# Reading x first, conditioning sums in four column groups on TensorE, and cact placed in front of x

## The reference

```
c_act = jax.nn.silu(c)
for l in range(DEPTH):
    mod = jnp.einsum('bd,kde->kbe', c_act, ada_w[l]) + ada_b[l][:, None, :]
    sh1, sc1, gt1 = jnp.split(mod[0], 3, axis=-1)
    sh2, sc2, gt2 = jnp.split(mod[1], 3, axis=-1)
    h = modulate(x, norm_mix_g[l], sh1, sc1)      # rmsnorm(x, g) * (1 + scale) + shift
    x = x + gt1[:, None, :] * token_mixer(h, ...)
    h = modulate(x, norm_ffn_g[l], sh2, sc2)
    x = x + gt2[:, None, :] * (swiglu or moe_ffn)(h, ...)
return rmsnorm(x, final_norm_g)
```

## Time and profile before

| | us |
|---|---|
| median of 3 runs | 1609.29 (1606.48 to 1611.79) |
| profiled execution | 1608.77 |
| its span, first to last instruction | 1606.8 |
| mean granted TensorE clock | 0.977 |
| PE busy | 1534.2 |
| DVE busy | 1174.7 |
| ACT busy | 785.8 |

### The profile page before, as it was taken

How to read it: one execution, slowest core, us unless ns; L and a number is a source line. 1 busy time by engine, 2 the same in 40 slices (tenths; PEclk the granted TensorE clock), 3 DMA queues, 4 the chain that set the end, 5 groups by cost and what they waited for, 6 DMA issues and landing times.

```text
span 1606.8 us, 22402 instructions
## 1 busy us (share of the span) xinstructions
PE 1534.2 (95%) x8920; PEld 1212.1 (75%) x8920; DVE 1174.7 (73%) x1451; ACT 785.8 (49%) x919; POOL 61.5 (4%) x49
## 2 busy tenths in 40 slices
PE   6899999999999999998999999799999999999993
PEld 6567877777888888886678768588888888888883
DVE  6777876766666565546578764589989998998994
ACT  2444236332222222214542463477777777777774
POOL 8200000000000000000000000100000000000001
PEclk9999999989999999999999999899999999999996
DMA  8362211436555564531211005299999999999975
GB/s 344 105 236 81 93 53 54 157 131 185 183 183 183 181 193 147 184 109 53 62 46 53 27 28 185 90 379 405 388 390 394 392 390 386 381 390 392 393 277 170
DMA packets 94454, 340.31 MB, mean 212 GB/s; under 512 B 10000, under 2 KB 14096, under 8 KB 91664
## 3 DMA queue, kind: packets, MB, share of 16 engines
q1 hardware_dynamic: 92048, 330.51, 56.8%
q0 software_dynamic: 2304, 8.39, 1.4%
HBM read 316.84 MB, written 22.02 MB: 211 GB/s over the span
## 4 chain that ended last, share of the span: by engine, by line
PE 90%; DVE 4%; DMA 2%; ACT 1%; issue 1%; POOL 0%; SPq 0%; POOLq 0%; ACTq 0%; DVEq 0%
PE ps L623 34%; PE ps L1194 10%; PE ps L1192 10%; PE ps L1193 10%; PE ps L924 2%; DMA scr<-in_ada 2%; DVE scr L1678 2%; PE ps L952 1%; PE ps L781 1%; PE ps L773 1%; PE ps L936 1%; PE ps L580 1%; PE ps L1034 1%; PE ps L636 1%; PE ps L1036 1%
## 5 line engine op out<-in xcount | busy, mean ns | idle before, releaser
L1675 DVE TENSOR_TENSOR wlm<-rawm,hlo 128x2048 fp32r<-128x2048 f32 x120 | 274.7, 2289 | 26.3 <-ACT hlo L1293 24.6
L1233 ACT ACTIVATE whi<-raw 128x1024 fp32r<-128x1024 f32 (+1 forms) x112 | 123.3, 1103 | 310.0 <-PE ps L623 265.1
L1293 ACT ACTIVATE hlo<-rawm 128x2048 fp32r<-128x2048 f32 x120 | 230.0, 1917 | 75.3 <-PE ps L1194 75.2
L623 PE MATMUL ps<-hhi,whi 128*128 128x512 f32 x624 | 257.0, 412 | 1.9 <-DVE wlo L1685 1.9
L1685 DVE TENSOR_TENSOR wlo<-raw,whi 128x1024 fp32r<-128x1024 f32 (+1 forms) x112 | 145.0, 1295 | 147.7 <-ACT whi L1233 145.4
L623 PE MATMUL ps<-hhi,wlo 128*128 128x512 f32 x624 | 247.1, 396 | 0.0
L623 PE MATMUL ps<-hlo,whi 128*128 128x512 f32 x624 | 246.1, 394 | 0.0
L1193 PE MATMUL ps<-wlm,xgh 128*128 128x512 f32 x480 | 187.7, 391 | 0.0
L1675 DVE TENSOR_TENSOR wlm<-rawm,whm 128x2048 fp32r<-128x2048 f32 x60 | 137.6, 2293 | 28.6 <-ACT whm L1293 28.6
L623 PEld LDWEIGHTS ps<-hhi,whi 128*128 128x128 f32 x624 | 117.9, 189 | 41.0 <-issue 12.8
L1192 PE MATMUL ps<-hlo,xgh 128*128 128x512 f32 x360 | 143.5, 399 | 0.6 <-issue 0.6
(11 more groups left out here) (315 smaller groups left out, 2553.0 us busy)
## 6 DMA issues: line engine op xcount, KB each, us to landing
rawm<-in_wm SPq DMA_DIRECT2D x360, 512.0 KB, 7.3
raw<-in_w SPq DMA_DIRECT2D x96, 512.0 KB, 3.6
adah<-in_ada SPq DMA_DIRECT2D x56, 512.0 KB, 4.3
scr<-in_ada SPq DMA_DIRECT2D x20, 1024.0 KB, 5.9
raw<-in_w SPq DMA_DIRECT2D x16, 704.0 KB, 4.1
xs<-scr SPq DMA_DIRECT2D x15, 512.0 KB, 5.4
ys<-yb SPq DMA_DIRECT2D x15, 512.0 KB, 8.4
xg<-xs SPq DMA_DIRECT2D x14, 512.0 KB, 7.0
```

Source lines behind the costliest of these rows:

```text
L623: ins = pe.matmul(ps[:, b, :], a, r[:, k0 + k, :], start=(start and first and k == ks[0] and n == 0), stop=(stop and last and k == ks[-1] ...
L1233: act.activation(whi[:, slot, 0:width], raw[:, slot, 0:width], ACT.Copy).then_inc(sem("hi_ready"), 1)
L1293: act.activation(hi_pair(q), raw_pair(q), ACT.Copy).then_inc(sem("him_ready"), 1)
L1675: return dve.tensor_tensor(out, a, b, op)
```

## The change

1. The first constants (identity, ones, and two columns moved to the front, `pick`, which is 1 on every 32nd partition, and `eps`) and `x` are issued ahead of the ada groups; all eight ada groups have buffers of their own and follow without a wait; the rest of the constants comes behind weight tiles 0 and 1. What reads those waits for `cst_in` at 32.
2. All eight groups are summed on PE. `condition_rows` multiplies with the stationary operand a column of `cact` repeated 32 times and the moving operand 256 columns of `ada`; chunk `k` goes to column group `k % 4`, so that the four partial sums stand on partitions 0-31, 32-63, 64-95 and 96-127 of one bank. ACT copies the bank to SBUF, and `condition_sum` turns and sums it with `pick` (two fp32 matmuls of one column).
3. DVE adds the squares of chunks 0 to 6 pairwise (`square_added`); PE sums only the last two. Then DVE makes `x*rstd` for all chunks ahead of `mod`. Scale and shift follow together: ACT makes `hhi` from `h` with scale and bias, DVE makes the same value unrounded (`whole`) and subtracts `hhi`.
4. `cact` is allocated in front of `x` instead of behind `rstd`.
5. `ang_ready`, `tap0` and `tap1` are replaced by counts on other semaphores; the same instructions wait for the same ones.

```diff
-BY_PE = (0, 2, 5, G_GATE, G_FFN - 1)
+BY_PE = tuple(range(G_IN)) + (G_GATE, G_FFN - 1)
...
         par = sb("par", [N_PAR])
+        cact = sb("cact", [DC])
         x = sb("x", [DC, S])
...
         rstd = sb("rstd", [S])
-        cact = sb("cact", [DC])
...
+        def row_bank(g):
+            return ps[:, (3, 4, 5, 6, 0, 1, 3, 4)[g], 0:256]
+        def row_copy(g):
+            return scr[:, 4 * 1024 + g % 4 * 256:4 * 1024 + g % 4 * 256 + 256]
...
-            for g in range(G_IN - 1):
+            sp.dma_start(cst[:, 0:N_FIRST], consts[:, 0:N_FIRST]).then_inc(sem("cst_in"), 16)
+            sp.dma_start(x[:], xT.rearrange("(c p) s -> p c s", p=P)).then_inc(sem("x_in"), 16)
+            for g in range(G_IN):
                 load_ada(g)
-            sp.dma_start(cst[:, 0:N_CONST - 9], consts[:, 0:N_CONST - 9]).then_inc(sem("cst_in"), 16)
-            sp.dma_start(x[:], xT.rearrange("(c p) s -> p c s", p=P)).then_inc(sem("x_in"), 16)
-            load_ada(G_IN - 1)
             load_tile(0)
             load_tile(1)
+            sp.dma_start(cst[:, N_FIRST:N_CONST - 9], consts[:, N_FIRST:N_CONST - 9]).then_inc(sem("cst_in"), 16)
...
+            def condition_rows(g):
+                ada_landed(pe, g)
+                if g >= 6:
+                    pe.wait_ge(sem("ada_copied"), g - 5)
+                for k in range(DC):
+                    j = 32 * (k % 4)
+                    ins = pe.matmul(row_bank(g)[j:j + 32, :], cact[:, k:k + 1].broadcast_to([P, 32]),
+                                    adar(g)[:, k * 256:(k + 1) * 256], start=(k < 4), stop=(k >= 4))
+                ins.then_inc(sem("ada_rows"), 1)
+            def condition_sum(g):
+                pe.wait_ge(sem("ada_copied"), g + 1)
+                for m in range(2):
+                    ins = pe.matmul(ps[:, 7, 2 * g + m:2 * g + m + 1], row_copy(g)[:, m * P:m * P + P], C("pick"),
+                                    start=True, stop=True)
+                ins.then_inc(sem("ada_used"), 1)
...
-                    for g in BY_PE[:3]:
-                        ada_sum(g)
+                    pe.wait_ge(sem("cact_ready"), 1)
                     pe.wait_ge(sem("cst_in"), 16)
-                    for g in (1, 3):
-                        ada_sum(g)
-                    for k in range(DC):
-                        square_sum(0, k)
-                    for g in (4, 6, 7):
-                        ada_sum(g)
+                    for g in range(G_IN):
+                        condition_rows(g)
+                        if g == 2:
+                            summed_squares(0)
+                        if g:
+                            condition_sum(g - 1)
+                    condition_sum(G_IN - 1)
...
+            for g in range(G_IN):
+                act.wait_ge(sem("ada_rows"), g + 1)
+                if g >= 4:
+                    act.wait_ge(sem("ada_used"), g - 3)
+                act.activation(row_copy(g), row_bank(g), ACT.Copy).then_inc(sem("ada_copied"), 1)
+                if g == 2:
+                    rms(0)
             for g in range(2):
                 split(g)
-            rms(0)
...
-            for g in (1, 3, 4, 6, 7):
-                ada_groups((g,))
+            dve.wait_ge(sem("x_in"), 16)
+            for k in range(1, DC - 1):
+                square_added(0, k)
+            inverse(0)
+            for k in range(DC):
+                tt(h[:, k, :], x[:, k, :], rstd[:]).then_inc(sem("hn_ready"), 1)
             for g in range(2):
                 split(g)
             dve.wait_ge(sem("ada_used"), G_IN)
             modulation(0, 2 * G_IN, 0, 1)
-            inverse(0)
+            for k in range(DC):
+                whole = scr[:, 5 * 1024 + k * S:5 * 1024 + k * S + S]
+                link(dve.tensor_scalar(whole, h[:, k, :], sclg[:, 0, k:k + 1], mod[:, k:k + 1], ALU.mult, ALU.add))
+                dve.wait_ge(sem("hhi_ready"), k + 1)
+                tt(hlo[:, k, :], whole, hhi[:, k, :].bitcast(F32), ALU.subtract).then_inc(sem("h_ready"), 1)
```

More of the change, by code:

```diff
@@ L44 @@
 _at = 0
-for _n, _w in (("ident", 128), ("ones", 128), ("bones", 128), ("rot", 128), ("istk", 64), ("amask", 256),
+for _n, _w in (("ident", 128), ("ones", 128), ("pick", 1), ("eps", 1), ("bones", 128), ("rot", 128), ("istk", 64), ("amask", 256),
                ("lev", 6 * 64), ("reset", 512), ("rows", 512), ("spread", 8 * 64), ("selg", 256),
                ("heads", 4 * 8), ("comb_r", 8), ("comb_l", 8), ("col_r", 16), ("col_l", 16), ("col_g", 16),
-               ("sign", 1), ("qscale", 1), ("rotm", 1), ("nrotm", 1),
-               ("eps", 1), ("before", 128), ("blocks", 16 * 8), ("rank", 8), ("invf", 1)):
+               ("sign", 1), ("qscale", 1), ("rotm", 1), ("nrotm", 1), ("before", 128), ("blocks", 16 * 8), ("rank", 8), ("invf", 1)):
     C_COLS[_n] = (_at, _at + _w)
@@ L52 @@
 N_CONST = _at
+N_FIRST = C_COLS["eps"][1]
 P_COLS = {}
@@ L115, in constants @@
     put("ones", np.ones((P, P)))
+    put("pick", (p % 32 == 0)[:, None] * 1.0)
     same = (p[:, None] // 64 == p[None, :] // 64)
@@ L395, in load_ada @@
                     sp.wait_ge(sem("sincos"), 2)
-                if g == 7:
-                    sp.wait_ge(sem("ada_used"), 1)
-                elif g == G_GATE + 2:
+                if g == G_GATE + 2:
                     sp.wait_ge(sem("ada_used"), G_GATE + 1)
@@ L553, in _ @@
                                         ALU.add, ALU.min))
-                pool.tensor_scalar(ang[:, n, :], ang[:, n, :], -float(np.float32(3.1415925)), None, ALU.max)\
-                    .then_inc(sem("ang_ready"), 1)
+                turn(pool.tensor_scalar(ang[:, n, :], ang[:, n, :], -float(np.float32(3.1415925)), None, ALU.max))
             pool.wait_ge(sem("xs_cleared"), 16 * NB)
@@ L895, in _ @@
                 for t in range(I_FILL):
+                    if t == 2:
+                        pe.wait_ge(sem("cst_in"), 32)
                     pe.wait_ge(sem(f"bank_free{t % 2}"), U_IN[layer] + t // 2)
@@ L1257, in shifted @@
                     shift = mod[:, s * 24 + k:s * 24 + k + 1]
-                    if s < 3:
+                    if s == 0:
+                        act.activation(hhi[:, k, :], h[:, k, :], ACT.Identity, scale=sclg[:, 0, k:k + 1], bias=shift)\
+                            .then_inc(sem("hhi_ready"), 1)
+                    elif s < 3:
                         act.activation(hhi[:, k, :], h[:, k, :], ACT.Identity, bias=shift).then_inc(sem("hhi_ready"), 1)
@@ L1416, in _ @@
                         if layer == 0:
-                            act.wait_ge(sem("ang_ready"), 2)
+                            act.wait_ge(sem("ang_step"), 2 + 2 * 13)
                             act.activation(sinb[:], ang[:, 2, :], ACT.Sin).then_inc(sem("sincos"), 1)
@@ L1726, in ada_first @@
                 if g >= 4:
-                    dve.wait_ge(sem("ada_used"), {4: 1, 6: 2, 7: 5}.get(g, max(G_IN, g - 3)))
+                    dve.wait_ge(sem("ada_used"), max(G_IN, g - 3))
                 return dve.tensor_scalar(adac[:, g % 4, :], w, cact[:, 0:1], None, ALU.mult)
@@ L1887, in _ @@
                     tap_list += [(d, 1)] + ([(d + lead, 0)] if d + lead < CV_K else [])
+                tap_at = {tap: n + 1 for n, tap in enumerate(tap_list)}
                 def taps(m):
@@ L1897, in taps @@
                         else:
-                            dve.wait_ge(sem(f"tap{n}"), CV_K * layer + d)
+                            dve.wait_ge(sem("tap"), 2 * CV_K * layer + tap_at[d - 1, n])
                             ins = stt(o[:, d:], src[:, :S - d], w, o[:, d:])
-                        ins.then_inc(sem(f"tap{n}"), 1)
+                        ins.then_inc(sem("tap"), 1)
                 def state(n):
@@ L2014, in _ @@
                         taps(2 * CV_K)
-                        for n in range(2):
-                            dve.wait_ge(sem(f"tap{n}"), CV_K * v)
+                        dve.wait_ge(sem("tap"), 2 * CV_K * v)
                         dve.sem_inc(sem("taps_done"), 1)
```

18 lines of the change are left out of this document (10 added, 8 removed).

## The result

| | before | after |
|---|---|---|
| median of the runs, us | 1610.60 (6 runs, 1606.48 to 1613.21) | 1598.42 (6 runs, 1593.27 to 1600.74) |
| ratio | | 0.9919, 95% interval 0.9905 to 0.9933 |
| profiled execution, its span | 1608.77, 1606.8 | 1593.27, 1591.2 |
| PE busy, us | 1534.2 | 1514.1 |
| TensorE clock granted, mean | 0.977 | 0.973 |

The change makes the kernel faster by 12.2 us, 0.8%. The forecast was 1584, that is 25 us faster; the time lies in its range (1577 to 1601), and the gain is a little less than half of what it said. The profiled execution after is the fastest of its six, so a comparison of the two profiles shows 15.5 us where the medians show 12.2.

The account below looks back on a forecast made before the run. The prediction took PE, busy 95% of the span, as the bound, with one long wait at the start. Its sum was 1608.8 - 8 (start) - 17 (address) = 1583.8, so 1584 us, range 1577 to 1601.

Parts of the forecast that it names:

- The start: Stretch up to `first_pair`: reordered transfers and sums on PE bring its first matmul to 42 instead of 50.2 us, gain 8.
- The pace of `first_pair`: In `first_pair`, behind the start: per chunk PE needs two triples, 1.40 us at full clock, and DVE 0.7 + 0.7.
- a rival: Conditioning sums at the start: column groups don't run together, 1601, or 1641 if PE also falls to half clock; chance 0.02.
- The weighing of the shared ports: DVE beside GpSimd at the start: trace shows slowing by a third to a half; full blocking would make the gain nearer 5.
- The address: Triples moving `hhi` or `hlo`: from byte 32 to 0 of 64 saves 20 ns each, 13.5 us plus 3.5, together 17.
- a term whose reason doesn't hold: Expert stage, 480 triples reading two of three moving operands from `hlo`: at most 6.4 us, half taken, 3.5.
- something else: Expert stage: whatever keeps `whm2`, at 0 of 64 already, at 0.69 a triple, not 0.68; it takes a part of the gain.
- the start alone: Whole kernel: the 20 ns belong to something else, such as a place above 100,000 bytes; 1601 us, chance 0.14.
- the one of the address alone: Whole kernel: DVE locked by POOL, or late products, leave at most 2 us of the start's gain; 1591 us, chance 0.06.
- the first case: Whole kernel: both gains, start and address, come; 1584 us, between 1577 and 1591, chance 0.76.
- The lines of 16 bytes: SBUF addresses 32224 and 32256: both are multiples of 16, so by the skill's rule the 32-byte shift brings nothing.

Follow-up runs that it names:

- start_only: The changed kernel with `cact` put back behind `rstd`, so new start and old address: 1600.11 us, ratio 0.9937.
- warm: The changed kernel with 15 matmuls added whose result nobody reads, to keep TensorE busy up to `first_pair`: 1600.54 us in one run.
- pool_late: The changed kernel with the second half of GpSimd's chain of angles held until both weight splits are done: 1600.29 us in one run.
- triples_idle: Bench of nothing but triples, operand addresses changed from group to group, other engines idle: 700 ns at the addresses before, 697 after, 680 at those of `ghi` and `glo`.
- addr_only: The kernel before with only `cact` moved in front of `x`, old start kept: 1603.80 us, ratio 0.9950.
- the repeat: The changed kernel as it is, measured once more on the same chip: 1597.85 us, ratio 0.9911.
- aligned: The changed kernel with `sclg` (128 bytes) put in front of `x` too: 1582.33 us, ratio 0.9818.

## Why the prediction was right and wrong

**The start: right.** Forecast were the first matmul at about 42 (bounds 39.3 to 45) and a gain of 8; measured 41.83 and 8.4. In `start_only` they are 41.03 and 9.2, with 8.7 left at 90 us, and its median says 11.4 with an interval from 6 to 14. The parts: squares begin at 12.3 (forecast: `x` there at 12.2), rows of a group 1.07 us (1.0) and `condition_sum` 0.5 to 0.6 (0.5) at full clock, copy 0.38 (0.4), both splits 3.70 (3.75). Two terms were off and cancelled. The last ada group's rows ended only at 34.5 instead of 33.6, since the clock was at half from 29.7 on and they took 1.91 us, where I had 1.0; and from the end of the splits to the first matmul it took 2.3 us, where I had 3.2. That they cancelled was luck. The pace of `first_pair` was off too: the prediction gave DVE 1.4 us a chunk, and it takes 2.3 with GpSimd beside it (`warm`). The clock I had not put into this stretch at all, only into a rival.

**The weighing of the shared ports: the trace was the better guide.** The Trainium skill, page "SBUF — State Buffer", section "SBUF: two separate sides", has the loser block fully for a whole instruction, by which the gain would have been nearer 5. Measured was 8.4. `pool_late` gives the price of GpSimd beside the two splits, 3.70 - 2.36 = 1.34 us, 0.67 for each, less than one of the GpSimd instructions beside them (1.49 and 1.26 us). That they hinder each other is thus shown; that each DVE instruction waits a whole one out is not, and whether it waits out the rest of one or is slowed all along, no run here tells.

**The address: this is the step that failed.** The prediction put it as "it looks as if 2048 bytes that start in the middle of a block of 64 are read as 33 blocks instead of 32", and took 20 ns for each of 752 triples, 13.5 us, plus 3.5 in the expert stage. What the runs showed in its place:

- The 20 ns are real, and they are the address's (`triples_idle`: 700 and 680 with all else at rest). On multiples of 32 bytes they hang on the distance between moving tile and weights modulo 256 bytes, not on the place in 64 bytes. The change moved the distance from 96 to 128, which is worth 3 ns a triple, not 20: 752 x 3 = 2.3 us where 13.5 stood. In the dense FFN, where 327 triples lie between the two rows of the table, 1.09 us were measured, 3.3 ns each. (The count of 752 leaves out 32 triples of the gate tiles, L983 before, 0.1 us at this price.)
- The expert stage gave 3.45 us, in `addr_only` as in the changed kernel. The forecast had 3.5, but as half of a term whose reason doesn't hold, so the size was luck. What the trace shows is 697 to 687 ns for the triples on `hlo`, which in the bench too is what a triple with two moving tiles at distance 128 and one at 0 takes.
- Start 8.4, dense triples 2.3 and expert stage 3.45 make 14.1 us; measured were 12.2 and, in the repeat, 13.6. The address alone brought 7.7 us by its medians (5 to 11), where the forecast had 17.

The two kinds of rows that the conjecture came from, `hhi` and `ghi`, differ in place modulo 64, modulo 256, in region and in distance from each other, and I chose the first because 6.7 ns are just 16 columns. A third kind of row spoke against it: `whm2`, at 0 of 64, had 0.69 and not 0.68. I saw it, called it "something else" and gave it half of a small term. It should have lowered the chance of the whole term. The rival "the start alone" was given 0.14 and is the one that came closest, with 1601 against 1598.42, though not by its own example: a place above 100,000 bytes isn't needed for 680. The measured time lies in the range only because the range was drawn up to 1601 for half of that rival and for the one of the address alone; the first case by itself ended at 1591.

**The lines of 16 bytes.** The Trainium skill, section "Specifications (TRN2)" of the same page, gives lines of 16 bytes, by which, as the prediction worked it out, a shift of 32 would bring nothing. As to the changed kernel that was nearly so, 3 ns of 20. As a rule it doesn't hold: with both moving tiles on whole lines of 16 bytes the triple still takes from 680 to 704 ns by the distance, and `aligned` gains 16 us over the changed kernel by 128 bytes (by medians; the slopes of the traces, 13 ns for each of 752 triples and 3.8 us in the expert stage, account for 13 to 14).

## What to carry to other kernels

Where two buffers differ in speed under the same instruction, list every way in which their addresses differ, the distance to the other operand among them, and ask for a third buffer that tells them apart before a term is put on it; a bench that runs some 40 address pairs in one launch of 0.74 ms tells apart what a rebuilt kernel, which changes one pair, leaves open. Where matmuls change their weights each time and stream 512 fp32r columns, let moving tile and weights start at the same place modulo 256 bytes, on multiples of 32: here that was 128 bytes of layout for 16 us. And before an idle engine or a low clock is mended, look whether its neighbour sets the pace: keeping TensorE's clock up through the start took 15 added matmuls and gave nothing that shows in the time.

## What the hardware showed that I had not expected

- A matmul of 512 fp32r columns with new weights takes 226.7 to 234.7 ns from start to start, by the distance of its operands modulo 256 bytes (0: 226.7; 64: 229; 96: 233.3; 208: 234.7), at a granted clock of 1.00, with nothing else at work and the weights at 128 of 256. Off multiples of 32 bytes distance 0 took 690 ns a triple in one run and 700 in another.
- A triple at a bad distance slows good ones behind it: `whm` 692 and 694 ns beside bad neighbours, 680 beside good ones. Four one-column matmuls between do the same: the next triples took 0.79, 0.69, 0.70 and 0.69 us in `aligned` before 0.68 was back.
- Loads at 222 GB/s, VectorE copies and ScalarE copies beside it cost such matmuls nothing that shows (218 in 50 us in each phase).
- Eight fp32 matmuls of 256 columns took 1.07 us on four column groups in turn and 3.70 on the whole array.
- In the stretch of layer 0's mixer that takes 26.0 us in one execution and 29.3 to 30.9 in others, the granted clock is 0.93 against 0.83 to 0.78, with the same busy time on VectorE and ScalarE.
